# Four weight buffers at four addresses modulo 128 bytes, in a two-block transformer kernel

## The reference, cut to what matters

```python
def swiglu(h, w_gate_up, w_down):
    gate, up = jnp.split(h @ w_gate_up, 2, axis=-1)
    return (jax.nn.silu(gate) * up) @ w_down

def sq_relu_mlp(x, w1, w2):
    return jnp.square(jax.nn.relu(x @ w1)) @ w2
```

## Time and profile before

| | |
|---|---|
| median of 3 runs | 3723.42 us (3721.8 to 3726.22) |
| profiled execution | 3725.33 us |
| its span | 3723.1 us |
| TensorE busy | 3346.2 us, 90% of the span, 20836 matmuls |
| VectorE busy | 1878.6 us, 50% |
| ScalarE busy | 1524.6 us, 41% |
| mean granted clock of TensorE | 0.936 |

### The profile page before, as it was taken

How to read it: one execution, slowest core, us unless ns; L and a number is a source line. 1 busy time by engine, 2 the same in 40 slices (tenths; PEclk the granted TensorE clock), 3 DMA queues, 4 the chain that set the end, 5 groups by cost and what they waited for, 6 DMA issues and landing times. The chain is left out here.

```text
span 3723.1 us, 52512 instructions
## 1 busy us (share of the span) xinstructions
PE 3346.2 (90%) x20836; PEld 2883.2 (77%) x20836; DVE 1878.6 (50%) x2682; ACT 1524.6 (41%) x2371; POOL 97.3 (3%) x158
## 2 busy tenths in 40 slices
PE   6999989789999799998889887985899989887998
PEld 4887758458877588776589777985699879886897
DVE  5444362654444533245555536656465566553655
ACT  4443342444433322233344424543363445442543
POOL 0000004000000000003000000000000000000000
PEclk8999989899999999999899978997899989996999
DMA  5544334024444222344145423543155435441452
GB/s 186 169 149 157 107 108 123 5 79 158 158 159 136 72 97 98 106 136 108 45 145 181 136 79 103 190 140 106 46 181 193 132 122 186 163 135 57 127 191 91
DMA packets 451670, 470.92 MB, mean 126 GB/s; under 512 B 8372, under 2 KB 446212, under 8 KB 451490
## 3 DMA queue, kind: packets, MB, share of 16 engines
q1 hardware_dynamic: 446608, 456.16, 38.1%
q0 software_dynamic: 4160, 11.95, 1.3%
q10 hardware_dynamic: 722, 0.29, 0.0%
HBM read 467.20 MB, written 1.20 MB: 126 GB/s over the span
## 5 line engine op out<-in xcount | busy, mean ns | idle before, releaser
L399 DVE TENSOR_TENSOR w_lo<-w_raw,w_hi 128x1024 fp32r<-128x1024 f32 x878 | 1062.8, 1225 | 1451.5 <-ACT w_hi L396 1448.9
L396 ACT ACTIVATE w_hi<-w_raw 128x1024 fp32r<-128x1024 f32 x878 | 912.2, 1056 | 1496.6 <-PE bank L409 1418.4
L407 PE MATMUL bank<-a_hi,w_hi 128*128 128x256 f32 (+1 forms) x3864 | 1250.0, 324 | 133.8 <-DVE a_lo L1456 37.5
L408 PE MATMUL bank<-a_lo,w_hi 128*128 128x256 f32 (+1 forms) x3864 | 1241.9, 321 | 0.0
L409 PE MATMUL bank<-a_hi,w_lo 128*128 128x256 f32 (+1 forms) x3864 | 1240.6, 321 | 0.0
L407 PEld LDWEIGHTS bank<-a_hi,w_hi 128*128 128x128 f32 x3864 | 751.9, 195 | 197.3 <-issue 97.9
L408 PEld LDWEIGHTS bank<-a_lo,w_hi 128*128 128x128 f32 x3864 | 752.2, 195 | 48.5 <-issue 0.5
L409 PEld LDWEIGHTS bank<-a_hi,w_lo 128*128 128x128 f32 x3864 | 751.1, 194 | 49.6
L407 PE MATMUL bank<-h_hi,w_hi 128*128 128x256 f32 (+1 forms) x1728 | 544.8, 315 | 0.0
L409 PE MATMUL bank<-h_hi,w_lo 128*128 128x256 f32 (+1 forms) x1728 | 539.9, 312 | 0.0
L408 PE MATMUL bank<-h_lo,w_hi 128*128 128x256 f32 (+1 forms) x1728 | 539.9, 312 | 0.0
(11 more groups left out here) (263 smaller groups left out, 2483.4 us busy)
## 6 DMA issues: line engine op xcount, KB each, us to landing
w_raw<-in_mlp_w SPq DMA_DIRECT2D x128, 1024.0 KB, 5.2
w_raw<-in_w_ffn_gate_up SPq DMA_DIRECT2D x88, 1024.0 KB, 5.1
w_raw<-in_w_mod SPq DMA_DIRECT2D x72, 1024.0 KB, 5.1
w_raw<-in_w_ffn_down SPq DMA_DIRECT2D x32, 1024.0 KB, 5.2
w_raw<-in_gla_w_in SPq DMA_DIRECT2D x24, 1024.0 KB, 5.2
w_raw<-in_w_in SPq DMA_DIRECT2D x16, 1024.0 KB, 5.6
w_raw<-in_ple_w_gate SPq DMA_DIRECT2D x16, 1024.0 KB, 5.0
w_raw<-in_w_ffn_down SPq DMA_DIRECT2D x16, 768.0 KB, 4.8
```

Of the source, the lines that this page charges most:

```text
L396: e.activation(hi, raw, ACT.Copy).then_inc(S.hi_ready.sem, 1)
L399: e.tensor_tensor(lo, raw, hi.bitcast(F32), ALU.subtract).then_inc(S.lo_ready.sem, 1)
L407: e.matmul(dst, hi, rhs_hi, start=start, stop=False)
L408: e.matmul(dst, hi, rhs_lo, start=False, stop=False)
```

## The change

Each of the two buffers of `w_hi` and of `w_lo` gets 4 elements (16 bytes) more, which no instruction touches: the tensor is allocated as [P, CUT, DK * SC + 4] and viewed in its old shape. `stat` grows from 24 to 40 elements, also unused. No instruction, wait or transfer is added, removed or moved.

```diff
-        w_hi = sb("w_hi", [P, CUT, DK, SC], F32R)
-        w_lo = sb("w_lo", [P, CUT, DK, SC], F32R)
+        w_hi = sb("w_hi", [P, CUT, DK * SC + 4], F32R)[:, :, 0:DK * SC].rearrange("p b (k c) -> p b k c", c=SC)
+        w_lo = sb("w_lo", [P, CUT, DK * SC + 4], F32R)[:, :, 0:DK * SC].rearrange("p b (k c) -> p b k c", c=SC)
...
-        stat = sb("stat", [P, 24])
+        stat = sb("stat", [P, 40])
```

## The result

The changed kernel takes 3750.42 us, median of 4 runs (3749.83 to 3751.34), beside 3723.27 us (3721.8 to 3726.22) of the kernel before on the same chip: a ratio of 1.0072, 95% interval 1.006 to 1.0084. It is slower by 27.2 us. I had said 3711 and faster or same; the time lies inside the range, on the other side of zero. The profiled execution has a span of 3747.6 us, 24.5 more than before.

What follows compares the result with a forecast made beforehand. TensorE was taken as the bound, its matmul count times the step. Gains of 26.0 us less losses of 14.2 gave -11.8 from 3723, so 3711 us; the 8-in-10 range was 3672 to 3754.

Steps and rivals of the forecast that it cites:

- What bounds the kernel: TensorE, busy 90% of the span: time is matmul count times start-to-start distance; VectorE and ScalarE wait for it.
- That the address makes the 113.3 and 120.0 ns: 256-column matmuls: `a`, at the weights' address modulo 128, steps 120.0 ns; `h`, at 64, 113.3, because of the addresses.
- no change: Rival: the place of `a` and `h` in memory makes the 6.7 ns, so nothing moves; 3723 us, chance 0.22.
- The cycle of 128 bytes: Addresses count modulo 128 bytes; `stat` makes the whole shift 128, so `h` and `z` stay at 64.
- The price of a mixture: Weights 16 to 48 bytes from the moving operand: 116.2 ns at 256 columns, 229.3 at 512, taken from modulation slots.
- my two thirds: Only two thirds of each group's matmuls were counted as moving, for gains of 26.0 and losses of 14.2 us.
- One load in three of all keeps its present price: In even slots `w_hi` keeps its address and is two of each three weight loads, so those matmuls keep their distance.
- The slower rival: Triples load from addresses 32 bytes apart, so no state settles: +31 us, 3755 (from 3731 up), chance 0.25.
- turning point: The slower case decides if the 256-column steps of `a` fall by less than 3 ns.
- Even and odd slots: Steps depend on slot parity: even slots nearer the old distances, odd ones changed more.
- Much faster: Rival: only equal starts cost, so `a` with 256 columns leaves 120.0 ns; 3657 to 3690 us, chance 0.18.
- The 53 us: Most that `a` with 256 columns could gain: 7848 matmuls times 6.7 ns.

Runs made afterwards that it cites:

- pad_256: Against the kernel before: each `w_hi` and `w_lo` buffer 64 elements (256 bytes) longer in place of the change's 4, `stat` as before; 3723.06 us, ratio 1.0004.
- rest_moved: Against the kernel before: weight buffers stay, only what lies behind them moves as in the change, `stat` at 40 elements; 3736.42 us, ratio 1.0036.
- both_moved: Against the kernel before: `h` used 64 bytes further at 512 columns and `a` 192 bytes further at 256 columns; 3691.99 us, ratio 0.9917.
- steps_by_address: Kernel without the network: only streams of matmuls, operands filled once, start addresses of weights and moving operand varied by 16 to 960 bytes; 564.43 us.
- steps_in_mixtures: Second kernel of matmul streams alone: the change's address offsets, offsets of 4 to 12 bytes, and streams like a modulation slot; 316.28 us.
- a_narrow_moved: Against the kernel before: `a_hi` and `a_lo` used 192 bytes further where only 256 columns are in use; 3697.25 us, ratio 0.9939.

## Why the prediction was wrong, point by point

- **What bounds the kernel**: right. TensorE's steps carry some 20 of the 24.5 us between the spans, the converters' durations stayed (1226 and 1056 ns), and pad_256 shows that nothing acts but addresses modulo 256.
- **That the address makes the 113.3 and 120.0 ns**: right, and now shown with streams alone. Its rival "no change" is out.
- **The cycle of 128 bytes, "`h`, `z` and the other regions stay at 64"**: wrong. The cycle is 256, and `h` moved from 64 to 192, which alone costs 14 us (rest_moved). I had two classes of operand and no row that told 128 from 256, and should have carried it as a bound.
- **The price of a mixture**, 116.2 and 229.3 ns from the modulation slots, is the step of the prediction that failed, and it turned the sign. Measured were 118.1 and 233.2 for `a`, 117.8 and 231.4 for `h`; with these prices and my two thirds the sum would have been +13 us. Those slots load 4 columns, and streams of such loads at one fixed address take 113.3 ns at 15 of 16 offsets: they don't feel the distance as full loads do, and were a poor neighbour. With the load moving 16 bytes each k, as in the kernel, the mean was 116.1, 120.0, 113.3 or 114.9 ns by where it began, so even for such slots 116.2 is the price of one place and not of a mixture. For 512 columns I had no row at all and copied the offset of the other width; of the 15 distances other than 0 in the table none is below 228.3, and at (0, 32) and (16, 48) it is 233.2 to 233.3.
- **"One load in three of all keeps its present price"**: wrong. A stream's triples share one pattern of steps. With only `w_lo` moved by 32, a stream of 512 columns takes 233.3 ns on average, not 226.7 for two matmuls of three. So the losses fall on all 3744 and 3600 matmuls: 3744 x 6.19 = 23.2 us and 3600 x 4.34 = 15.6 us where I had 7.2 and 7.0, while the large gain is 7848 x 1.84 = 14.4 us in place of 19.9. With `h` at 512 columns (2.9) and the weights as moving operand (1.7) the sum becomes +19.8 in place of -11.8. With 0.7 of the modulation slots, some 4 us of the 24.5 between the spans stay unassigned by this sum. The granted clock of the two profiled executions was 0.936 and 0.935; a thousandth of 3748 us, some 4 us, is my estimate of what that could make, and no run separates it.
- **The slower rival** was the nearest, and in part by luck. It had the right size in the group that it decides, 21 us for `a` with 512 columns, measured 21.7, and the state at 226.7 ns is indeed lost. Its mechanism, that a triple's loads must lie apart for that, is not needed: streams with both loads 16, 32 or 48 bytes from the moving operand take 233.3 ns, as do those of (0, 32) and (16, 48). `h` with 256 columns lost 15.4 where it had 10, `a` with 256 columns gained 12.5 where it had 0, and its 3755 came out as 3750. Its turning point, a fall of less than 3 ns in `a` with 256 columns, was met: 1.8. My range held the time only because it took in half of this rival.
- **Even and odd slots** differ little (streams of 118.2 and 117.8 ns), as both mixtures are bad; the modulation slots stayed near their 1.86 us (steps of 115.8 and 116.4 ns), as I had said. **Much faster** (3654 by its own sum, though I wrote from 3657) failed because 16 to 48 bytes are a better place than 0 by no more than 2.2 ns at 256 columns. The 53 us were there, at 64, and the steps of both_moved take 36 of them (899.0 to 863.2 us in that group).

The Trainium skill (SBUF — State Buffer, Who interferes with whom) has TensorE waiting on nobody, which made the sum 0. The traces disagree: with 512 columns the step grew by 6.2 ns of 227 in the kernel and by 6.6 in streams with no other engine at work; whether that is a wait for memory or something inside TensorE these runs don't tell.

## What to carry to other kernels

Where back-to-back fp32r matmuls with a 128x128 weight load each bound a kernel, the difference of the two operands' addresses modulo 256 bytes is a parameter worth up to 3% of a step at 512 columns and 6% at 256. Here 0 was best for 512 columns and 64 for 256, for `hi` and `lo` alike, though at 64 the pace was sometimes 117.8 ns and not 113.3; the whole kernel gained 0.8% (both_moved). Choose the difference by measurement and read it off the built program, since a small tensor that grows shifts all behind it. Spreading buffers over different addresses is not a cure by itself: of the 16 distances only 64 lies below 116 ns at 256 columns, and only 0 below 228 at 512. A price taken from another shape, here 4-column loads for 128-column ones, belongs into the range and not into the sum; short streams of the shape in question settle it in one run.

## What the runs showed that I had not expected

- Two settled paces at one and the same distance: at 64 a stream of 256 columns took 113.3 ns in steps_by_address and 117.8 in steps_in_mixtures. In the kernel each held for a whole stretch of up to 816 matmuls, and the first part of `h` behind it kept the pace of the `a` before, the later parts not always. It may be what makes a_narrow_moved vary from 3690 to 3709 us, which is not shown, as only the execution of 3690 has a trace; what picks the pace, and how to force the better one, is open.
- Offsets of less than 16 bytes count, so the steps do not go by lines of 16 bytes, as I had thought possible for steps_in_mixtures: distances of 4, 8 and 12 bytes took 118.2, 115.6 and 116.7 ns at 256 columns and 232.6, 230.9 and 233.3 at 512.
- The steadiest steps are whole multiples of 16 cycles of 2.4 GHz: 113.3 ns is 272 cycles, 120.0 is 288, 226.7 is 544 and 233.3 is 560, for 256 and 512 columns. At the half clock there is nothing over: 213 ns for 256 columns of `a`, before and after. The Trainium skill (TensorE: Matmul & The Clock Gate, section Wait — 56ns, not 53.3ns?) says that a fixed cost of 2.5 ns shows only at the 2.4 GHz clock. The trace agrees about the clock and not about the size, which is 6.7 to 13.3 ns at 256 columns and hangs on addresses.
- The two moving operands count apart too: with `a_lo` alone 64 bytes further, everything else at 0, a stream of 512 columns took 231.8 ns in place of 226.7.
